# Up matmuls of 512 columns as two of 256 with the same stationary operand, in a one-core decoder layer

## The chip, the cores and the metric

The kernel runs on one core of a Trainium2 chip. The metric is the device time of one execution in microseconds (us); lower is better. The runs of the kernel before gave 2425.76 us as median of three, from 2422.67 to 2427.23. One further execution was profiled: 2423.22 us, of which the span from the first to the last instruction is 2421.1 us.

## What is computed

One decoder layer over 256 tokens of width 2048 in float32. After the attention part comes a product-key layer with 128 x 128 = 16384 single-neuron experts. This case concerns its last step:

```python
u = expert_down[et]
h = jax.nn.gelu(jnp.einsum('cd,ced->ce', xt, u), approximate=False)
vv = expert_up[et]
return jnp.einsum('ce,ced->cd', gt * h, vv)
...
h = layer_norm(ALPHA * h + y_p, ln2_g[l], ln2_b[l])
```

Each token has 128 chosen experts. The kernel doesn't gather their rows for this sum. It puts the gate values into a dense matrix G over all 16384 experts (zero where an expert isn't chosen), computes the activation A of every expert, and multiplies the product M = A * G (16384 x 256) with `expert_up` (16384 x 2048).

## The kernel before

Everything that is multiplied is streamed from HBM in tiles of 128 x 2048 float32 (two halves of 1024 columns, 512 KB each), through four raw slots. To keep float32 accuracy each number is taken apart into a high part, rounded to the format fp32r, and a low part, the rest. ScalarE (ACT) makes the high part (line 455), VectorE (DVE) the low part (line 765), and TensorE (PE) makes three products: high by high, high by low, low by high. The sync engine (SP) issues the loads (line 336).

The stages follow each other on TensorE in the order of the program:

- The projections, the attention and the query projection use `full` and `up_proj`. There the weight block of 128 x 128 is the stationary operand and the tokens are the moving one, 256 columns wide (line 1274, helper `three`). In the query projection (16 tiles, `r_hi` and `r_lo`) the moving operand has 258 columns.
- The down stage, 128 tiles in a loop of 16 passes with 8 tiles each, has pairs of a matmul of 480 columns (line 1468 or 1472) and one of 240 columns (line 1469 or 1471), 16 pairs a tile.
- The up stage, 128 tiles, turns the operands round: the stationary one is a block of M, 128 experts by 128 tokens (`m_hi`, `m_lo`, one for each half `tt` of the tokens), and the moving one is the expert tile in the weight slots. The result, 256 x 2048 float32, stays in the accumulator memory PSUM for the whole stage: it fills all eight banks of 512 columns. `up` (line 1493) takes a tile in two halves `hf` of 1024 columns, each by both `tt`, by three products `q`, by two chunks `c` of 512 columns: 24 matmuls a tile. Both chunks of a product have the same stationary operand. `first` is the first tile: it takes `tt` 1 first, since the accumulators of the down stage lie where `tt` 0 is written, and its `start` flag clears the bank ahead of the first product.

The first 8 tiles of the up stage are written out, then comes a loop of 14 passes with 8 tiles each, then 6 tiles written out. These are 126 tiles by `up`. The last two tiles go by `up_bank`, bank after bank, so that the final normalization can begin. The second half of a tile (from the third tile on) has its parts in the memory of `a_all`, which the down stage no longer needs; the first half has them in `w_first`.

In front of each tile TensorE waits for `mlo_ready` (the block of M is ready) and in front of each half for `lo_ready`. The last matmul of a half gives `half_used`, on which ACT and DVE wait to refill a slot, DVE also to make the next block of M (lines 1172, 1177, with ACT's line 673 between them).

Of the kernel before, what the change touches and what calls it, by code (L numbers as in the profile page):

```python
# [34 lines left out]
D = 2048  # L35
# [29 lines left out]
HALF = 1024  # L65
# [76 lines left out]
def build(nc, stream, x_t, const_in, small_in, keys_t, ln2, rows_dram, y_out, a_dram, g_dram):  # L142
# [92 lines left out]
    ps = ctx.enter_context(nc.psum_tensor("ps", [P, 8 * 512], F32))  # L235
# [43 lines left out]
    def weights(t, hf, moved=False):  # L279

        return (up_hi[:, t.par, :], up_lo[:, t.par, :]) if moved and hf else (w_hi[t.slot(hf)], w_lo[t.slot(hf)])
# [982 lines left out]
    def _(pe):  # L1264
        pe.sem_inc(half_used, HALVES_FREE)

        def half_ready(t, hf):
            pe.wait_ge(lo_ready, t.half(hf) + 1 + HALVES_FREE)
# [171 lines left out]
        for g in range(8):  # L1440
            tt, c0 = g % 2, 4 * (g // 2)
# [3 lines left out]
            for c in range(4):  # L1445
                ins = pe.matmul(spare[g % 4][:, P * c:P * c + P], qp[:, c0 + c, P * tt:P * tt + P], keys[:, (c0 + c) % 2, :],  # L1446
                                start=True, stop=True)
            ins.then_inc(sc_mm, 1)
        for g in range(8):
            tt, c0 = g % 2, 4 * (g // 2)  # L1450
            pe.wait_ge(sc_ready, g + 5) if g < 4 else pe.wait_ge(ht_ready, g - 3)
            pe.wait_ge(h1_ready, c0 + 4)
            for c in range(4):
                ins = pe.transpose(spare[g % 4][:, P * c:P * c + P], res[:, c0 + c, P * tt:P * tt + P], ident)
# [25 lines left out]
        def up(t, n, b, moved=True, first=False):  # L1480
            pe.wait_ge(mlo_ready, n + 1)
            for hf in range(2):
                half_ready(t, hf)
                high, low = weights(t, hf, moved)
                for tt in (1, 0) if first else range(TT):
                    s = slice(P * tt, P * tt + P)
                    if first and hf == 0 and tt == 0:
                        for u in (Tile(T_UP - 2), Tile(T_UP - 1)):
                            pe.wait_ge(acc_free[u.par], u.pair + 2)
                    for q, (m, w) in enumerate(((m_hi, high), (m_hi, low), (m_lo, high))):  # L1490
                        for c in range(2):
                            o = D * tt + HALF * hf + 512 * c
                            ins = pe.matmul(ps[:, o:o + 512], m[:, b % 2, s], w[:, 512 * c:512 * c + 512],  # L1493
                                            start=first and q == 0, stop=False, skip_group_check=True)
                ins.then_inc(half_used, 1)

        def up_bank(t, b, tt, c):

            s = slice(P * tt, P * tt + P)
            o = D * tt + 512 * c  # L1500
            w = slice(512 * (c % 2), 512 * (c % 2) + 512)
            high, low = weights(t, c // 2, True)
            pe.matmul(ps[:, o:o + 512], m_hi[:, b % 2, s], high[:, w], start=False, stop=False, skip_group_check=True)
            pe.matmul(ps[:, o:o + 512], m_hi[:, b % 2, s], low[:, w], start=False, stop=False, skip_group_check=True)
            return pe.matmul(ps[:, o:o + 512], m_lo[:, b % 2, s], high[:, w], start=False, stop=False, skip_group_check=True)

        for b in range(8):
            up(Tile(T_UP + b), b, b, b > 1, b == 0)
        with pe.Fori(1, NKEYS // 8 - 1) as i:
            for b in range(8):  # L1510
                up(Tile(T_UP + b, i, 8), i * 8 + b, b)
        for b in range(6):
            up(Tile(T_UP + NKEYS - 8 + b), NKEYS - 8 + b, b)
        last = (Tile(N_TILES - 2), Tile(N_TILES - 1))
        for b, t in enumerate(last):
            pe.wait_ge(mlo_ready, NKEYS - 1 + b)
            for c in range(4):
                if c % 2 == 0:
                    half_ready(t, c // 2)
                ins = up_bank(t, b, 0, c)  # L1520
# [92 lines left out]
```

## Time and profile before

| | |
|---|---|
| runs of the kernel before | 2422.67 to 2427.23 us, median 2425.76 us |
| profiled execution | 2423.22 us, span 2421.1 us |
| granted TensorE clock | 0.998 |
| TensorE matmul (PE) busy | 2398.4 us, 99% |
| TensorE weight load (PEld) busy | 2202.7 us, 91% |
| DVE, ACT, POOL busy | 65%, 49%, 24% |
| chain of work that ended last | 99% TensorE; line 1274 38%, line 1493 29%, line 1468 17% |

The end of a matmul in the trace is modelled: a row of 390 ns for a matmul doesn't mean that the next one starts 390 ns later. Where matmuls follow each other, the pace is the distance from start to start, or a stretch of time divided by the matmuls in it. A timeline row merges several matmuls ("x4") and gives the start of the first. PEld is the load of a stationary operand; each matmul has one, also where the operand is the same as before.

### The profile page before, as it was taken

To read this page: it belongs to the slowest core of one execution; us is meant where nothing else is said; L and a number is where in the kernel's file an instruction comes from. 1 tells how busy PE (TensorE), PEld (TensorE's weight loads), DVE (VectorE), ACT (ScalarE), POOL (GpSimd) and SP (SyncE) were. 2 spreads that over 40 slices of the span, in tenths; PEclk is the share of its full clock that TensorE was granted. 3 is DMA by queue.
4 is the path that set the end of the run, shared out by engine and by line. 5 is a ranking of instruction groups with operands and counts; after the bars stand their busy time and mean duration, and the time that the engine had idled before them with its cause. 6 is when DMAs were issued, how large, how long until landed. Compare 5 with 4: busy or idle time off the path is not lost.

```text
span 2421.1 us, 45160 instructions
## 1 busy us (share of the span) xinstructions
PE 2398.4 (99%) x15884; PEld 2202.7 (91%) x15884; DVE 1567.7 (65%) x2615; ACT 1196.5 (49%) x1787; POOL 589.8 (24%) x427
## 2 busy tenths in 40 slices
PE   8999999999999999999999999999999999999997
PEld 8999999999999999999999999999888888888886
DVE  5555555546666666888878887755655555555556
ACT  4444444545454444665556565444444444444444
POOL 0000000000000000487568886786000000000000
PEclk9999999999999999999999999999999999999999
DMA  7667666564545665688788899988776677677764
GB/s 271 217 218 227 214 230 207 182 195 149 164 148 174 194 196 178 200 219 229 220 262 259 251 275 292 280 222 260 243 244 232 236 244 243 232 238 242 243 232 145
DMA packets 182918, 539.01 MB, mean 223 GB/s; under 512 B 53664, under 2 KB 53664, under 8 KB 180432
## 3 DMA queue, kind: packets, MB, share of 16 engines
q1 hardware_dynamic: 124128, 449.89, 56.2%
q0 software_dynamic: 54128, 71.68, 12.0%
q10 hardware_dynamic: 4608, 16.78, 2.3%
q8 instruction: 26, 0.43, 0.1%
q14 instruction: 28, 0.23, 0.0%
HBM read 501.42 MB, written 35.78 MB: 222 GB/s over the span
## 4 chain that ended last, share of the span: by engine, by line
PE 99%; DVE 1%; DMA 0%; ACT 0%; issue 0%; DVEq 0%
PE ps L1274 38%; PE ps L1493 29%; PE ps L1468 17%; PE ps L1469 9%; PE ps L1472 1%; PE ps L1313 1%; PE ps L1471 1%; PE ps L1328 1%; PE ps L1321 0%; PE ps L1315 0%; PE ps L1446 0%; PE ps L1329 0%; PE ps L1308 0%; DVE u_s L1227 0%; DVE u_s L1237 0%; DVE y_s L1214 0%
## 5 line engine op out<-in xcount | busy, mean ns | idle before, releaser
L765 DVE TENSOR_TENSOR w_first<-raw,w_first 128x1024 fp32r<-128x1024 f32 x425 | 520.8, 1225 | 366.7 <-ACT w_first L455 364.6
L390 POOL DMA_INDIRECT g_dram<-lists x256 | 439.3, 1716 | 98.4 <-issue 81.8
L455 ACT ACTIVATE w_first<-raw 128x1024 fp32r<-128x1024 f32 x425 | 447.4, 1053 | 1.5 <-DMA raw<-stream 0.6
L765 DVE TENSOR_TENSOR w_second<-raw,w_second 128x1024 fp32r<-128x1024 f32 x299 | 365.9, 1224 | 2.2 <-ACT w_second L455 2.1
L1468 PE MATMUL ps<-a_all,w_first 128*128 128x480 f32 x1024 | 345.7, 384 | 0.0
L1274 PE MATMUL ps<-a_all,w_first 128*128 128x256 f32 x2520 | 314.5, 281 | 9.0 <-DVE w_first L765 9.0
L455 ACT ACTIVATE w_second<-raw 128x1024 fp32r<-128x1024 f32 x299 | 314.4, 1052 | 2.9 <-DMA raw<-stream 2.5
L1274 PEld LDWEIGHTS ps<-a_all,w_first 128*128 128x128 f32 x2520 | 299.0, 189 | 10.0 <-issue 9.0
L1274 PE MATMUL ps<-a_all,w_second 128*128 128x256 f32 x2520 | 304.5, 277 | 0.2 <-DVE a_all L796 0.2
L1468 PE MATMUL ps<-a_all,w_second 128*128 128x480 f32 x896 | 302.1, 382 | 0.0
L1274 PEld LDWEIGHTS ps<-a_all,w_second 128*128 128x128 f32 x2520 | 294.5, 188 | 0.4 <-DVE a_all L796 0.4
L1469 PE MATMUL ps<-a_all,w_first 128*128 128x240 f32 x1024 | 278.4, 272 | 0.0
L1493 PE MATMUL ps<-w_first,m_hi 128*128 128x512 f32 x1008 | 270.9, 391 | 0.0
L1493 PE MATMUL ps<-a_all,m_hi 128*128 128x512 f32 x992 | 266.5, 390 | 0.0
L765 DVE TENSOR_TENSOR a_all<-raw,a_all 128x1024 fp32r<-128x1024 f32 x126 | 154.6, 1227 | 156.7 <-ACT a_all L455 156.7
L1469 PE MATMUL ps<-a_all,w_second 128*128 128x240 f32 x896 | 243.9, 272 | 0.0
L1493 PEld LDWEIGHTS ps<-w_first,m_hi 128*128 128x128 f32 x1008 | 189.2, 188 | 41.7
L1493 PEld LDWEIGHTS ps<-a_all,m_hi 128*128 128x128 f32 x992 | 186.3, 188 | 41.0
L455 ACT ACTIVATE a_all<-raw 128x1024 fp32r<-128x1024 f32 x126 | 133.4, 1059 | 177.3 <-PE ps L1493 177.3
L1468 PEld LDWEIGHTS ps<-a_all,w_first 128*128 128x128 f32 x1024 | 192.6, 188 | 28.0
L1469 PEld LDWEIGHTS ps<-a_all,w_first 128*128 128x128 f32 x1024 | 194.0, 189 | 4.3
L678 ACT ACTIVATE part<-ps 128x240 f32<-128x240 f32 x128 | 47.7, 373 | 295.5 <-PE ps L1472 295.5
(230 smaller groups left out, 3519.7 us busy)
## 6 DMA issues: line engine op xcount, KB each, us to landing
raw<-stream SPq DMA_DIRECT2D x850, 512.0 KB, 4.3
g_dram<-blank POOLq DMA_DIRECT2D x32, 512.0 KB, 6.1
a_dram<-act ACTq DMA_DIRECT2D x32, 512.0 KB, 3.7
a_in<-a_dram POOLq DMA_DIRECT2D x32, 512.0 KB, 5.1
g_in<-g_dram POOLq DMA_DIRECT2D x32, 512.0 KB, 6.3
g_dram<-lists POOLq DMA_INDIRECT x256
res<-x_t SPq DMA_DIRECT2D x4, 512.0 KB, 6.8
ln_s<-ln POOLq DMA_DIRECT2D x1, 2048.0 KB, 7.1
```

Source lines behind the costliest of these rows:

```text
L390: pool.indirect_dma_start(out=g_cell, out_offset=bass.IndirectOffsetOnAxis(ap=lists[0:n, tt, 1, j, c:c + 1], axis=0), in_=lists[0:n, tt, 2 ...
L455: act.activation(weights(t, hf, moved)[0], raw[:, t.slot(hf), :], ACT.Copy).then_inc(hi_ready, 1)
L678: act.activation(part[:, t.par, :], acc[t.par][:, DENSE:2 * DENSE], ACT.Copy).then_inc(part_ready, 1)
L765: dve.tensor_tensor(low, raw[:, s, :], high.bitcast(F32), ALU.subtract).then_inc(lo_ready, 1)
L1274: ins = pe.matmul(out, w, a, start=first and q == 0, stop=last and q == 2)
L1313: ins = pe.matmul(ps_s[:, o:o + k1], q_s[:, q0:q0 + P], k_s[:, 0:k1], start=True, stop=not rope)
L1328: pe.matmul(ps_o[:, 0:T], v_s[:, 0, :], p_t[:, 0:T], start=True, stop=False, skip_group_check=True)
L1468: pe.matmul(both, wh, a_all[:, kk, 0:2 * DENSE], start=kk == 0, stop=False)
L1469: ins = pe.matmul(high, wl, a_all[:, kk, 0:DENSE], start=False, stop=False)
L1471: pe.matmul(high, wl, a_all[:, kk, 0:DENSE], start=False, stop=False)
L1472: ins = pe.matmul(both, wh, a_all[:, kk, 0:2 * DENSE], start=False, stop=True)
L1493: ins = pe.matmul(ps[:, o:o + 512], m[:, b % 2, s], w[:, 512 * c:512 * c + 512], start=first and q == 0, stop=False, skip_group_check=True)
```

## The change

In `up`, each matmul of 512 columns becomes two of 256 columns that follow each other, with the same stationary operand, into the two halves of the same bank. In the first tile the `start` flag, which clears the whole bank, stands only on the first of the two; the second writes where the bank has been cleared. The last matmul of a half still gives `half_used`. `up_bank` isn't changed, nor any other engine's program.

```diff
                     for q, (m, w) in enumerate(((m_hi, high), (m_hi, low), (m_lo, high))):
-                        for c in range(2):
-                            o = D * tt + HALF * hf + 512 * c
-                            ins = pe.matmul(ps[:, o:o + 512], m[:, b % 2, s], w[:, 512 * c:512 * c + 512],
-                                            start=first and q == 0, stop=False, skip_group_check=True)
+                        for c in range(4):
+                            o = D * tt + HALF * hf + 256 * c
+                            ins = pe.matmul(ps[:, o:o + 256], m[:, b % 2, s], w[:, 256 * c:256 * c + 256],
+                                            start=first and q == 0 and c % 2 == 0, stop=False, skip_group_check=True)
                 ins.then_inc(half_used, 1)
```

TensorE's order where the loop of the down stage ends and the first tile of the up stage begins, before:

```order
L1475 COMPARE_AND_BRANCH
L1493 MATMUL ps<-w_first,m_hi 128x512 x4
L1493 MATMUL ps<-w_first,m_lo 128x512 x2
L1493 MATMUL ps<-w_first,m_hi 128x512 x4
L1493 MATMUL ps<-w_first,m_lo 128x512 x2
L1493 MATMUL ps<-w_second,m_hi 128x512 x4
```

and now:

```order
L1475 COMPARE_AND_BRANCH
L1493 MATMUL ps<-w_first,m_hi 128x256 x8
L1493 MATMUL ps<-w_first,m_lo 128x256 x4
L1493 MATMUL ps<-w_first,m_hi 128x256 x8
L1493 MATMUL ps<-w_first,m_lo 128x256 x4
L1493 MATMUL ps<-w_second,m_hi 128x256 x8
```

Nothing has moved: each row has twice the matmuls at half the width. In the text of the program TensorE has 3734 matmuls where it had 3206; the loop of the up stage has 384 of them in a pass of its body where it had 192.

## Rows read from the trace of the kernel before

**Rows 1.** The page: share of each engine, and the chain that ended last.
```profile
PE 2398.4 (99%) x15884; PEld 2202.7 (91%) x15884; DVE 1567.7 (65%) x2615; ACT 1196.5 (49%) x1787; POOL 589.8 (24%) x427
...
PE 99%; DVE 1%; DMA 0%; ACT 0%; issue 0%; DVEq 0%
```

**Rows 2.** The chain from 1704 us on: start us, us, what.
```profile
1704.43 692.29 PE ps L1493 x3024
```

**Rows 3.** Stretches of 60 us in the up stage, line 1493 alone; columns as named.
```profile
core 0: us, PE busy (x) PEld busy (x), PEclk, DMA share, GB/s
1800.00:1860.00 60.00, 60.00 (x264) 49.24 (x263) 1.00 0.71 240
2300.00:2360.00 60.00, 60.00 (x264) 49.23 (x263) 1.00 0.68 232
```

**Rows 4.** Timeline of PE in the attention output projection: start us, us, engine, line.
```profile
801.74 2.88 PE L1274 MATMUL ps<-a_all,w_first 128*128 128x256 f32 x24
804.46 0.62 PE L1274 MATMUL ps<-a_all,w_second 128*128 128x256 f32 x4
```

**Rows 5.** Timeline of PEld at the same place: the weight loads.
```profile
801.63 2.79 PEld L1274 LDWEIGHTS ps<-a_all,w_first 128*128 128x128 f32 x24
804.35 0.64 PEld L1274 LDWEIGHTS ps<-a_all,w_second 128*128 128x128 f32 x5
```

**Rows 6.** Timeline of PE in the query projection, 258 columns.
```profile
945.37 0.28 PE L1274 MATMUL ps<-r_lo,w_first 128*128 128x258 f32 x1
...
946.93 0.28 PE L1274 MATMUL ps<-r_hi,w_first 128*128 128x258 f32 x1
```

**Rows 7.** Timeline from the last down tile into the first up tile, all engines.
```profile
1698.98 0.38 PE L1468 MATMUL ps<-a_all,w_first 128*128 128x480 f32 x1
...
1703.83 0.27 PE L1469 MATMUL ps<-a_all,w_second 128*128 128x240 f32 x1
...
1703.94 0.27 PE L1471 MATMUL ps<-a_all,w_second 128*128 128x240 f32 x1
...
1704.05 0.38 PE L1472 MATMUL ps<-a_all,w_second 128*128 128x480 f32 x1
...
1704.27 1.12 PE L1493 MATMUL ps<-w_first,m_hi 128*128 128x512 f32 x4
...
1704.87 0.41 DVE L1117 TENSOR_TENSOR part<-ps,part 128x240 f32<-128x240 f32 x1 [0.40 <-ACT part L678]
...
1705.68 1.08 PE L1493 MATMUL ps<-w_first,m_hi 128*128 128x512 f32 x4
```

**Rows 8.** Waits within 1750 to 2390 us: engine, line waited for, us, times, longest.
```profile
ACT m_hi L673 <- DVE m_f L1172: 190.6, 117, 1.6
ACT a_all L455 <- PE ps L1493: 164.9, 116, 1.5
DVE a_all L765 <- ACT a_all L455: 146.9, 117, 1.3
```

**Rows 9.** Timeline where the loop of the up stage begins, all engines.
```profile
1745.34 0.42 DVE L1172 TENSOR_TENSOR m_f<-a_in,g_in 128x256 f32<-128x256 f32 x1
...
1746.24 0.42 DVE L1177 TENSOR_TENSOR m_lo<-m_f,m_hi 128x256 fp32r<-128x256 f32 x1 [0.48 <-ACT m_hi L673]
...
1748.34 1.07 PE L1493 MATMUL ps<-w_first,m_hi 128*128 128x512 f32 x4
```

**Rows 10.** The page's DMA queues: packets, MB, share of 16 engines.
```profile
q8 instruction: 26, 0.43, 0.1%
```

## The prediction

> **What bounds the kernel now.** I began with the page. TensorE is busy 99% of the span and holds 99% of the chain that ended last [rows 1]. The reader is to see there that only the pace of TensorE can move the time by much, and that a busy share of 99% says nothing about that pace. The chain has one piece for the whole of `up`: 3024 matmuls in 692.29 us, without a gap [rows 2]. The count is right, 126 tiles with 24 matmuls. So one matmul of 512 columns takes 692.29 / 3024 = **228.9 ns** from start to start. Two stretches of 60 us, 500 us apart, have the same count (264 each) at a granted clock of 1.00 [rows 3]: the pace is steady and no clock effect is in it.
>
> Next I asked whether anything feeds this stage late. DMA moves 232 to 240 GB/s at a share of about 0.7 [rows 3]. ACT's longest waits in this stage are for DVE and for TensorE itself: 164.9 us in 116 waits until a half has been used; DVE in its turn waits for ACT [rows 8]. The next block of M is ready at 1746.24 + 0.42 = 1746.66 us and is wanted at 1748.34 us, 1.7 us later [rows 9]. So everyone else waits for TensorE, and the stage is 3024 times the pace of a matmul.
>
> **The change, part by part.** It removes 3024 matmuls of 512 columns and adds 6048 of 256, each with its own load of the stationary operand. The one number wanted is the pace of a matmul of 256 columns in this place. The trace has no such matmul in the up stage, so I bound it by neighbours.
>
> The nearest row is the same shape elsewhere: fp32r, 128x128 stationary, 256 columns. In the output projection 24 matmuls start between 801.74 and 804.46 us: 2.72 us / 24 = **113.3 ns** [rows 4]. The operands differ (there the weights are stationary and the tokens move), and there all matmuls of a tile add to the same columns. The loads keep up: 24 loads start in 804.35 - 801.63 = 2.72 us too, at the same 113.3 ns [rows 5]. So a new load for every 256 columns has been carried at this pace, which matters, since the change doubles the loads from one in 228.9 ns to one in 113 ns. By this row two halves take 226.7 ns, 2.27 ns less than the one of 512: 3024 x (226.7 - 228.9) = **-6.9 us** (with 113.33 and 228.93 before rounding).
>
> The low bound is the matmul of 240 columns in the down stage: 0.11 us from the first one's start to the next, twice in a row [rows 7], so about 110 ns. Two halves can hardly be quicker than two of these: 220 ns, 3024 x (220 - 228.9) = -27 us. I don't take it, because it has 16 columns fewer, and a row with just 256 exists.
>
> The high bounds are three. First, the 258-column matmuls of the query projection: 13 of them in 946.93 - 945.37 = 1.56 us, 120.0 ns each [rows 6]. That is 6.7 ns more for 2 columns more. Two of those: 240.0 ns, 3024 x 11.1 = +34 us. Second, the down stage's cost for a column: a tile of 16 pairs runs from 1698.98 to 1704.27 us, 5.29 us / 16 = 330.6 ns for 720 columns, 0.459 ns a column [rows 7]; 256 columns make 117.6 ns, two 235.1 ns, 3024 x 6.2 = +19 us. Third, a straight line (fixed cost a, cost b for a column) through the up and the down stage: a + 512 b = 228.9 and 2a + 720 b = 330.6 give b = 0.418 ns and a = 14.7 ns. Then each added matmul costs 14.7 ns, 3024 x 14.7 = +44 us.
>
> Why I take 113.3 ns against that line: it would make 256 columns 121.8 ns, and the trace has thousands at 113.3. The 258-column row suggests a step just above 256 columns: cost doesn't grow evenly, and 256 lies on the cheap side of the step. If 480 and 512 columns lie beyond it and pay for it, all these rows agree without a cost for each instruction. That is a reading of four paces and not a mechanism that I can see.
>
> A rule of the Trainium skill speaks against the change. It has no part in the sum. TensorE: Matmul & The Clock Gate, section "Back-to-back issue gap", gives N / 2.4 + 2.5 ns for a matmul of N columns: 215.8 ns for 512 and 218.3 ns for two of 256. By that rule every added matmul costs 2.5 ns, 7.6 us in all, an estimate from that page. The trace doesn't have its figures: 228.9 and 113.3 ns are both above it, by 13.1 and 4.1 ns.
>
> **Edits at nothing.** The bank is changed after two matmuls instead of after one; both ways the next result goes elsewhere, and the stage ran at an even pace [rows 3]. The start of the stage: the first tile takes `tt` 1 first, 6 matmuls of 512 columns, and then needs what DVE reads of the down accumulators. DVE is done at 1704.87 + 0.41 = 1705.28 us and TensorE gets there at 1705.68 us [rows 7]. With 12 x 113.3 = 1.36 us instead of 1.37 us nothing changes; the cover is 0.4 us. What comes late next, if TensorE is quicker by 24 x 2.27 = 54 ns a tile: the block of M with its cover of 1.7 us [rows 9]. It isn't used up. DVE, ACT, POOL and SP have the same programs.
>
> Instructions: the body of the up loop grows from 192 to 384 matmuls; the largest body so far is the down loop's with 256. Code is fetched in packets, 26 of them in the run for 0.43 MB, at 0.1% of 16 engines' span: 0.001 x 16 x 2421 / 26 = about 1.5 us each [rows 10]. I put this at nothing, because the page's chain has 0% for issue [rows 1] although the program has loops of up to 256 matmuls.
>
> **The sum.** The profiled execution took 2423.22 us, 2.5 us under the median of the runs. Less 6.9 us it would be 2416.4 us; the median of 2425.76 us would be **2418.9 us**.
>
> **Rivals.**
> 1. *Cost by columns.* In this stage a column costs 228.9 / 512 = 0.447 ns, whatever the width. Then 256 columns take 114.5 ns and nothing changes: 2425.8 us. For it: between 256 and 512 columns the cost per column differs by 1% only (0.443 and 0.447 ns). Against it: 240 columns at 110 ns are 0.458 ns a column.
> 2. *The load beside the stream is dear here* (slower). Beside 512 columns a load is in work for part of the time: PEld is busy 49.2 of 60 us [rows 3]; now there is always one. If a matmul in this stage is slowed while the next operand comes in, 256 columns cost 117.6 to 120.0 ns, by the rows of the down stage and of the query projection: +19 to +34 us, 2445 to 2459 us. It decides from 114.5 ns on. Against it: in the projections the loads follow each other at 113.3 ns and the matmuls with them [rows 4, 5].
> 3. *A fixed cost for each matmul* (slower): 14.7 ns by the line through both stages, +44 us, 2470 us. Against it stand the 256-column rows, for it that both neighbours on the time axis lie on it.
> 4. *The jump back of a longer loop* (slower). If the body no longer stays on the chip, each of 13 jumps back waits for a packet, 13 x 1.5 = +20 us on top of the -6.9: 2439 us; if three packets each time, more. The Trainium skill bears on this in Runtime: NRT & Kernel Launch, section "Instruction fetch mechanics": a taken branch whose target isn't in the window stalls, but TensorE's instruction memory is given as 2048 instructions, and a body of 384 matmuls with their loads is under 800. By its size no stall would come; no run here has shown it.
>
> **How the numbers follow.** Forecast (113.3 ns): 0.52. Rival 1: 0.12. Rival 2: 0.16. Rival 3: 0.10. Rival 4: 0.10. About 0.2%, 4.9 us, is what a measurement of this kernel can tell from no change. The forecast's gain is 0.28%, so I leave 0.04 of its 0.52 to "same": faster 0.48, same 0.17, slower 0.35. The range goes from 2413 us (a little more than the forecast's gain) to 2452 us: that takes in rival 1, rival 4 and the lower half of rival 2, and leaves out rival 3, the upper half of rival 2 and a gain toward the 240-column bound, together under 0.2. The forecast's own range is 2415 to 2421 us.
>
> **What would show it.** In the profile after, the chain should have 6048 matmuls on line 1493 in about 685.4 us: 113.3 ns each, 529 or 530 starts in a stretch of 60 us, weight loads at the same pace, no idle time of TensorE. Rival 1 is right if the piece stays at 692 us. With rival 2 or 3 the pace is an even 118 to 122 ns with nobody waited for. With rival 4 the pace within a pass is 113.3 ns, and a gap of over 1 us stands once in eight tiles, with more than 26 packets of code. ACT should still wait for TensorE in each tile. A clock under 1.00 in the stage, or a shift in the other stages, would make the prediction wrong in a way that I don't foresee.

## The result and the profile after

| | before | after |
|---|---|---|
| time, us | 2424.22, median of 4 runs (2422.27 to 2427.23) | 2442.89, median of 4 runs (2442.51 to 2446.23) |
| profiled execution, us | 2423.22 | 2443.16 |
| its span, us | 2421.1 | 2441.0 |
| mean granted clock | 0.998 | 0.998 |

The changed kernel is slower by 0.84%: the ratio of its time to the time before is 1.0084, with a 95% interval of 1.0073 to 1.0096, or 18 to 23 us. I had forecast a gain of 6.9 us.

The page after, its row of engines and its chain (they answer to [rows 1]):

```profile
PE 2418.3 (99%) x18908; PEld 2346.9 (96%) x18908; DVE 1567.3 (64%) x2615; ACT 1196.7 (49%) x1787; POOL 592.8 (24%) x427
...
PE 99%; DVE 1%; DMA 0%; ACT 0%; issue 0%; DVEq 0%
```

TensorE has 3024 matmuls more and nothing else has changed on this level: it still holds 99% of the span and of the chain. The chain from 1704 us on (start us, us, what) shows where the time is; it answers to [rows 2]:

```profile
1704.27 712.35 PE ps L1493 x6048
```

The piece was 692.29 us and is 712.35 us: +20.06 us, and the profiled executions differ by 19.94 us. So the whole difference lies in this one piece, and the same sum shows that nothing else moved. One matmul of 256 columns takes 712.35 / 6048 = **117.8 ns** here; two take 235.6 ns, where the one of 512 took 228.9.

Stretches of the up stage after, line 1493 alone (columns as in [rows 3]: stretch, length, PE and PEld busy with counts, granted clock, DMA share, GB/s), and one stretch of the output projection, line 1274:

```profile
core 0: us, PE busy (x) PEld busy (x), PEclk, DMA share, GB/s
1800.00:1860.00 60.00, 60.00 (x512) 60.00 (x511) 1.00 0.67 228
2300.00:2360.00 60.00, 60.00 (x512) 60.00 (x511) 1.00 0.68 237
...
770.00:830.00 60.00, 60.00 (x532) 60.00 (x531) 1.00 0.59 193
```

The pace is even: 512 in both stretches of the stage (a count includes those that run over an edge). My forecast wanted 529 or 530 starts, and with the two at the edges that is the 532 of the projection, where the same shape runs as before. The clock is full in all three, so the two paces, 117.8 and 113.3 ns, are no matter of the clock.

Nobody feeds the stage late. In 1750 to 2400 us ACT waits for TensorE (us, times, longest) as in [rows 8], a little longer than the 164.9 us there, and the queue of code packets has 30 of them where [rows 10] has 26:

```profile
ACT a_all L455 <- PE ps L1493: 183.7, 116, 1.7
...
q8 instruction: 30, 0.49, 0.1%
```

The four packets more cost nothing that can be seen: the chain is one piece, issue has 0% of it, and there is no idle time of TensorE between passes of the loop. The rule that I had weighed in the prediction, of a stall at a taken branch whose target isn't in the window (the Trainium skill, Runtime: NRT & Kernel Launch, "Instruction fetch mechanics"), doesn't show here with a body of 384 matmuls.

The timeline at the stage's start (start us, us, engine, line), beside [rows 7]:

```profile
1704.11 1.13 PE L1493 MATMUL ps<-w_first,m_hi 128*128 128x256 f32 x8
...
1704.71 0.41 DVE L1117 TENSOR_TENSOR part<-ps,part 128x240 f32<-128x240 f32 x1 [0.40 <-ACT part L678]
...
1705.55 1.10 PE L1493 MATMUL ps<-w_first,m_hi 128*128 128x256 f32 x8
```

DVE is done at 1705.12 us and TensorE comes at 1705.55 us: the cover of 0.4 us held. But from 1704.11 to 1705.55 us 12 matmuls start, 120 ns each with the first, longer step: the pace is off from the first tile on.

So the question is why the shape that takes 113.3 ns in the projections takes 117.8 ns here.

### The profile page after: what moved, and what is told of

The parts are those of the page before. It is cut to its first block, busy times and chain, and to the rows that moved or that the text cites. A ratio compares the mean times of both kernels' runs of the same rounds, so it can differ in the third digit from the quotient of the medians.

```text
span 2441.0 us, 51208 instructions
## 1 busy us (share of the span) xinstructions
PE 2418.3 (99%) x18908; PEld 2346.9 (96%) x18908; DVE 1567.3 (64%) x2615; ACT 1196.7 (49%) x1787; POOL 592.8 (24%) x427
## 4 chain that ended last, share of the span: by engine, by line
PE 99%; DVE 1%; DMA 0%; ACT 0%; issue 0%; DVEq 0%
PE ps L1274 38%; PE ps L1493 29%; PE ps L1468 17%; PE ps L1469 9%; PE ps L1472 1%; PE ps L1313 1%; PE ps L1471 1%; PE ps L1328 1%; PE ps L1321 0%; PE ps L1315 0%; PE ps L1446 0%; PE ps L1329 0%; PE ps L1308 0%; DVE u_s L1227 0%; DVE u_s L1237 0%; DVE y_s L1214 0%
## 5 line engine op out<-in xcount | busy, mean ns | idle before, releaser
L1274 PEld LDWEIGHTS ps<-a_all,w_second 128*128 128x128 f32 x2520 | 294.2, 188 | 0.4 <-DVE a_all L796 0.4
L1493 PE MATMUL ps<-w_first,m_hi 128*128 128x256 f32 x2016 | 278.0, 279 | 0.0
L1493 PE MATMUL ps<-a_all,m_hi 128*128 128x256 f32 x1984 | 273.6, 279 | 0.0
L1493 PEld LDWEIGHTS ps<-w_first,m_hi 128*128 128x128 f32 x2016 | 255.0, 188 | 0.1
L1493 PEld LDWEIGHTS ps<-a_all,m_hi 128*128 128x128 f32 x1984 | 251.0, 188 | 0.0
L1468 PEld LDWEIGHTS ps<-a_all,w_second 128*128 128x128 f32 x896 | 168.6, 188 | 27.6
```

What stands on the lines that cost most here:

```text
L1274: ins = pe.matmul(out, w, a, start=first and q == 0, stop=last and q == 2)
L1468: pe.matmul(both, wh, a_all[:, kk, 0:2 * DENSE], start=kk == 0, stop=False)
L1493: ins = pe.matmul(ps[:, o:o + 256], m[:, b % 2, s], w[:, 256 * c:256 * c + 256], start=first and q == 0 and c % 2 == 0, stop=False, skip_g ...
```

## The experiments

### Is it the company, the form or the place?

Four theories stood at first; the letters are those of the expectations. A: every matmul has a fixed cost, 6.7 ns, and each column 0.434 ns (the line through 228.9 ns for 512 columns and 117.8 ns for 256). B: the company does it (transfers, other engines at work). C: the place of the results or of the operands sets the pace. D: the load of the stationary operand sets a floor.

**Probes on a quiet core.** Behind the last output, when no one else works, 24 matmuls each of one width, then variants of one thing at 512 and at 256 columns.

```diff
+        pe.wait_ge(out_ready, 4 * TT)
+        def probe(w, m, o, n, step=0, mstep=0, wstep=0, count=24):
+            for k in range(count):
+                oo, mo, wo = o + step * (k % 2), mstep * (k % 2), wstep * (k % 2)
+                pe.matmul(ps[:, oo:oo + n], w[:, wo:wo + P], m[:, mo:mo + n], start=True, stop=True, skip_group_check=True)
+        for n in (512, 480, 448, 384, 320, 288, 272, 258, 256, 240, 224, 192, 128, 64):
+            probe(mh, w_hi[0], 0, n)
...
+            probe(w_hi[0], a_flat[:, 0:1024], 0, n, wstep=128)
+            probe(mh, w_hi[0], 0, n, step=512, mstep=512, wstep=256)
```

> The kernel before, and behind its last output blocks of 24 matmuls each on a quiet core (no DVE, ACT or stream at work), one row of the timeline for each block; their results are used by nobody. First a sweep of widths from 512 to 64 columns with m_hi stationary and an expert tile moving, as in the up stage; then 512 and 256 columns with one thing changed at a time: destination bank alternating, moving operand alternating, stationary operand alternating, moving operand in other memory, stationary operand from a weight slot, all three alternating. Theory A (a fixed cost of 6.7 ns for each matmul and 0.434 ns for a column, the line through 228.9 ns for 512 and 117.8 ns for 256 columns in the up stage): 256 columns take 117.8 ns and 512 take 228.9 ns here too, 384 take 173 ns, 128 take 62 ns unless the load of the stationary operand needs more. Theory B (the 0.434 ns for a column come from what the other engines and the stream do to TensorE's reads or writes in the stage): on the quiet core 256 columns take 113.3 ns and 512 take 220 ns or less. Theory C (where the operands lie or whether the destination changes decides): one of the alternations or places moves 256 columns from 113.3 to 117.8 ns. Theory D (the load sets a floor): all widths under some 256 columns take the same 110 to 118 ns.

The groups of the sweep (by form: count, busy us, mean ns of one). Busy time covers 23 steps and one whole matmul, so the pace is (busy - mean) / 23:

```profile
L1532 PE MATMUL ps<-w_first,m_hi 128*128 128x480 f32 x24 | 5.4, 380 | 0.0
...
L1532 PE MATMUL ps<-w_first,m_hi 128*128 128x384 f32 x24 | 4.3, 336 | 0.0
L1532 PE MATMUL ps<-w_first,m_hi 128*128 128x320 f32 x24 | 3.7, 307 | 0.0
...
L1532 PE MATMUL ps<-w_first,m_hi 128*128 128x258 f32 x24 | 3.0, 282 | 0.0
L1532 PE MATMUL ps<-w_first,m_hi 128*128 128x256 f32 x24 | 3.0, 279 | 0.0
L1532 PE MATMUL ps<-w_first,m_hi 128*128 128x240 f32 x24 | 2.8, 274 | 0.0
...
L1532 PE MATMUL ps<-w_first,m_hi 128*128 128x128 f32 x24 | 2.8, 274 | 0.0
L1532 PE MATMUL ps<-w_first,m_hi 128*128 128x64 f32 x24 | 2.8, 276 | 0.0
```

That gives 218 ns for 480 columns, 172 for 384, 147 for 320, 118 for 258 and for 256, and 110 ns for 240, 128 and 64 alike (within 2 ns each). Two things are new. There is no step at 256 columns: 258 and 256 differ by no more than that reading's 2 ns. And from 240 columns down there is a floor of 110 ns. My low bound, 110 ns for 240 columns, was this floor.

The quiet core has the pace of the up stage: about 118 ns for the up stage's own operands at 256 columns, with no transfer under way (share 0.00). B falls. The variants, from the timeline (start us, us, line, count) of those that follow each other:

```profile
2526.53 14.24 PE L1532 MATMUL ps<-w_first,m_hi 128*128 128x512 f32 x96
2540.61 2.99 PE L1532 MATMUL ps<-w_second,m_hi 128*128 128x256 f32 x24
2543.43 5.87 PE L1532 MATMUL ps<-a_all,m_hi 128*128 128x256 f32 x48
2549.14 5.78 PE L1532 MATMUL ps<-a_all,w_first 128*128 128x256 f32 x48
2554.75 2.88 PE L1532 MATMUL ps<-w_first,m_hi 128*128 128x256 f32 x24
```

The row of 2540.61 has 24 starts in 2543.43 - 2540.61 = 2.82 us, 117.5 ns. The last row has the same kinds of operands as the first 256-column probes, and 23 steps in 2.88 - 0.28 = 2.60 us: 113 ns. **One form has two paces.** Changing one thing at a time (the bank of the result, the moving operand, the stationary operand) left 229 and 117.8 ns. The last row alternates all three at once, so the probes alone don't exclude that the combination does it; the swapped kernel below settles that. The two rows of 48 between them mix two probes each, and their means are 119.0 and 116.9 ns: a third pace, 120.0 ns, is in both, for the probes whose two operands start at the same offset within 128 bytes (the start of `a_all` with `m_hi`; `w_first` with the up stage's part of `a_all`, which begins 64 bytes behind its start). At 512 columns the same probes were the quicker ones. Two stretches of PE (columns: stretch, length, busy with count, clock, DMA share, GB/s), the first in such a probe, the second in one with `w_first` stationary and the start of `a_all` moving:

```profile
2511.00:2515.00 4.00, 4.00 (x20) 1.00 0.00 0
...
2523.00:2526.00 3.00, 3.00 (x14) 1.00 0.00 0
```

By the starts within them these are 226.7 ns and 233.3 ns. The operands of the second probe gave 113.4 ns at 256 columns: what is quick for one width is slow for the other. I come back to this below.

**All results into one place.** After, with every pass of the loop adding to the same 256 columns.

```diff
-                            o = D * tt + HALF * hf + 256 * c
+                            o = D * tt + HALF * hf + 256 * c if not one else 0
```

> The changed kernel, but in the 14 passes of the loop every matmul of the up stage adds into the same 256 columns of one bank, as a tile of the projections does (the sums of those 112 tiles are lost). Theory C, destination: 113.3 ns a matmul in the loop, 112 x 48 x 4.45 ns = 24 us less than the changed kernel, about 2417 us in the profiled execution. Theories A and B: 117.8 ns as before, 2441 us in span.

2446.38 us. The chain:

```profile
1707.38 712.35 PE ps L1493 x6048
```

The same 712.35 us: the place of the results isn't it.

**The roles swapped.** After, the loop's passes with the expert's tile stationary and M moving, as the projections have it.

```diff
+                            if swap:
+                                ins = pe.matmul(ps[:, o:o + 256], w[:, g:g + P], m[:, b % 2, :],
+                                                start=False, stop=False, skip_group_check=True)
```

> The changed kernel, but in the 14 passes of the loop the operands change roles: the expert tile is stationary in blocks of 128 x 128, the block of M moves with its 256 columns, as in the projections; 48 matmuls of 256 columns a tile as before (the loop's sums come out transposed, so in the wrong places). If the roles or the memory of the operands decide, 113.3 ns a matmul and about 24 us less than the changed kernel; if the stage's company decides (theory B), 117.8 ns and no change.

2417.52 us. The chain, with line 1498 for the normal roles (8 tiles ahead of the loop, 6 behind) and 1495 for the swapped ones:

```profile
1703.94 45.05 PE ps L1498 x384
1748.99 609.30 PE ps L1495 x5376
2358.29 32.64 PE ps L1498 x288
```

The first line is 117.3 ns a matmul, the second 113.3 ns, and the third, the old form again, 32.64 / 288 = **113.3 ns**. That fits neither A nor C: the form that was slow ahead of the loop is quick behind it. The pace is carried on from what ran before, as on the quiet core. The swapped form took only two matmuls to reach 113.3 ns.

The first line isn't one pace either. In the first two tiles the halves in `w_second` ran at 113.5 ns and everything else at 117.8 ns; on return to `w_first` the pace fell back.

**384 and 128 instead of 256 and 256.**

```diff
-                        for c in range(4):
-                            o = D * tt + HALF * hf + 256 * c
+                        for c, (at, n2) in enumerate(((0, 384), (384, 128), (512, 384), (896, 128))):
+                            o = D * tt + HALF * hf + at
```

> The change with other sizes: each 512 columns as 384 and 128. By theory A without a floor the two take 173.3 + 62.2 = 235.6 ns, as two of 256 do, and the time is that of the changed kernel, +20 us to before. With a floor of about 110 ns under each matmul (theory D) the pair takes 173 + 110 = 283 ns, 3024 x 54 ns = +164 us to before, about 2588 us.

2596.0 us, 173.5 us more than before beside it. The chain:

```profile
1702.57 866.85 PE ps L1493 x6048
```

The pair takes 286.7 ns; the probes gave 172 + 110 = 282 ns, and without a floor A wanted 235.6 ns. So 128 columns save nothing against 240: the floor holds in the stage too. A split with a narrow part is dear, at any pace.

### What decides which pace is held?

Theory E: the pace is a state that lasts while matmuls follow each other. The down stage leaves TensorE in the slow one, and a stop lets it enter the quick one. Theory F, which came later: there are two paces for one stream, a stop can end in either, and either lasts until something disturbs it.

**A short stop ahead of the stage**, with 256 and with 512 columns: TensorE waits for its own last matmul of the down stage.

```diff
             pe.wait_ge(mlo_ready, n + 1)
+            if first:
+                pe.wait_ge(half_used, Tile(T_UP - 1).half(1) + 1 + HALVES_FREE)
```

> The changed kernel with one more wait: ahead of the first matmul of the up stage TensorE waits until its own last matmul of the down stage has counted as done, a stop of some 0.2 to 0.4 us. Theory E (the pace is a state of TensorE's pipeline that lasts while matmuls follow each other: the down stage leaves it in a slow one, 117.8 ns for 256 columns, a stop lets it fall into the quick one, 113.3 ns): the whole stage runs at 113.3 ns, 6048 x 4.45 = 27 us less than the changed kernel and 6.9 us less than the kernel before, about 2417 us. Theory A (fixed cost for each matmul): 117.8 ns, 2443 us as the changed kernel.

2446.49 us, ratio 1.0087 (1.0070 to 1.0104); 712.56 us for the 6048 matmuls, the slow pace.

> The kernel before, matmuls of 512 columns, with the same one wait ahead of the up stage. Theory E: 512 columns have a quick pace too, 226.7 ns (seen once on the quiet core) in place of 228.9, 3024 x 2.27 = 6.9 us less than before, and some 0.3 us of stop: about 2417.5 us. Theory A: 228.9 ns, no change but the stop.

2426.55 us, ratio 1.0006 (0.9997 to 1.0016); 692.50 us, 229 ns. A short stop changes neither pace, against E.

**A longer stop**: the first tile in its natural order, so that TensorE waits about 1 us for the down accumulators to be read.

```diff
-                for tt in (1, 0) if first else range(TT):
+                for tt in range(TT):
```

> The changed kernel, the first up tile in the natural order of the token halves, so that TensorE waits about 1 us for the accumulators of the down stage to be read. Theory E: 113.3 ns from then on, about 2418 us. Theory A: 117.8 ns, about 2444 us.

2443.64 us. The timeline of TensorE behind the stop:

```profile
1704.73 1.15 PE L1493 MATMUL ps<-w_first,m_hi 128*128 128x256 f32 x8 [0.99 <-DVE part L1117]
1705.72 0.62 PE L1493 MATMUL ps<-w_first,m_lo 128*128 128x256 f32 x4
1706.17 1.07 PE L1493 MATMUL ps<-w_first,m_hi 128*128 128x256 f32 x8
...
1707.53 1.11 PE L1493 MATMUL ps<-w_second,m_hi 128*128 128x256 f32 x8
1708.47 0.63 PE L1493 MATMUL ps<-w_second,m_lo 128*128 128x256 f32 x4
```

From 1705.72 to 1707.53 us 16 matmuls start in 1.81 us: 113.1 ns. From 1707.53 on 8 start in 0.94 us: 117.5 ns. The quick pace was there for half a tile and was gone with the switch to `w_second`. It came back once, in the half of the second tile that lies in `w_second` (8 matmuls in 0.91 us from 1713.19 us on), and went with the next switch. Then the stage stayed slow; the piece is 712.36 us.

**Is it where w_second lies?** The same, with the gap of 128 bytes ahead of `w_second` moved behind it.

```diff
-    sb("gap_w", [P, 32])
     w_second = sb("w_second", [P, 2, 2, HALF], F32R)
+    sb("gap_w", [P, 32])
```

> The changed kernel with the long stop of about 1 us at the start of the up stage, which gave 113.3 ns until the first switch to w_second, and with the gap of 128 bytes between w_first and w_second moved behind w_second. Theory F with the offset as the disturbance: 113.3 ns through the first tiles and, if nothing else disturbs it, through the stage, about 2418 us. If the switch itself disturbs and not the offset: 117.8 ns from the second half of the first tile on. The other stages may change by a few us through the new addresses.

2440.74 us, 712.56 us for the piece: the slow pace from the first tile on. It didn't help. And the stop was the same 0.99 us, with the same operands at the same places behind it (`w_first` and `m_hi` haven't moved): the half tile that had 113.1 ns in the run before had 117.8 ns here, on another chip. So a stop of 1 us, too, was followed once by either pace.

**Pairs as in the down stage, put into a projection**: before, with 8 pairs of 480 and 240 columns between the second and third tile of a projection.

```diff
+        for k in range(8):
+            pe.matmul(ps_o[:, 0:480], a_all[:, k, 0:P], a_all[:, k + 1, 0:480], start=True, stop=True)
+            pe.matmul(ps_o[:, 0:240], a_all[:, k, P:2 * P], a_all[:, k + 1, 0:240], start=True, stop=True)
```

> The kernel before, with 8 pairs of a 480-column and a 240-column matmul put between the second and the third tile of the mix projection (their result goes to a bank that nobody reads); 2.6 us of work. There TensorE runs at 113.3 ns for 256 columns before and after. Theory E: behind the pairs the 256-column matmuls may stay at 117.8 to 120 ns until TensorE next stops, 14 tiles x 48 x 4.5 ns = +3 us on top of the 2.6. Theories A and C: 113.3 ns on both sides.

2429.45 us in one execution, 3.2 us more than the median of before beside it, whose own executions lie 6.7 us apart; so the timeline has to tell. The pairs alone take 2.6 us. They are 326 ns each, where the down stage has 330.6 ns (here both operands lie in `a_all`), so they weren't quite that stage's stream. Behind them:

```profile
851.38 0.28 PE L1274 MATMUL ps<-b_hi,w_first 128*128 128x256 f32 x1
...
851.97 0.39 PE L1274 MATMUL ps<-b_hi,w_first 128*128 128x256 f32 x2
...
852.99 0.28 PE L1274 MATMUL ps<-b_hi,w_first 128*128 128x256 f32 x1
```

Five matmuls start between 851.38 and 851.97 us, 118 ns each, and the next nine in 1.02 us, 113.3 ns. In a projection the quick pace is back after five matmuls, without a stop, as it was after two in the swapped kernel. E falls as I had put it: the slow pace doesn't last everywhere until TensorE stops. But projections aren't free of it, as the trace of the kernel before shows (further down).

### A stop inside the stage

**A wait of 2.5 us ahead of the third tile**, for the second half of the tile behind it.

```diff
             pe.wait_ge(mlo_ready, n + 1)
+            if isinstance(n, int) and n == 2:
+                half_ready(t.next(), 1)
```

> The changed kernel; TensorE stops ahead of the third up tile until a half of the fourth is ready, about 2.5 us. From that tile on only w_first and a_all are moving operands. Theory F (TensorE has two paces for one and the same stream of 256-column matmuls, 113.3 and 117.8 ns, either lasts until something disturbs it; the switch from w_first to w_second disturbs it, the switch from w_first to a_all does not): if the stop ends in the quick pace it stays for the 124 tiles that follow, 124 x 48 x 4.45 = 26.5 us less than the changed kernel, about 2419 us; a stop can also end in the slow one, as in the kernel with the short stop, then about 2446 us. What theory A (a fixed cost for a matmul) expects is 117.8 ns whatever is done.

2419.04 us in one execution, 3.6 us less than before beside it (2422.63, from 2420.25 to 2427.41). Timeline and chain:

```profile
1717.63 1.15 PE L1495 MATMUL ps<-w_first,m_hi 128*128 128x256 f32 x8 [2.51 <-issue]
...
1717.63 674.80 PE ps L1495 x5952
```

Here the whole rest of the stage, 124 tiles, ran at 674.80 / 5952 = 113.4 ns. The forecast's pace is possible in this stage, with its operands, its company and its loops.

**The same kernel again**, on another chip.

> The kernel with the stop of 2.8 us ahead of the third up tile again, timed in five rounds. Theory F, if the quick pace is entered each time: every execution near 2419 us, some 4 us under the kernel before in the same rounds, ratio 0.998. If the entry is left to chance from run to run: some executions at 2419 and some at 2446 us.

2446.83 us (2446.61 to 2447.02, 4 runs), ratio 1.0101 (1.0085 to 1.0118). Timeline ahead of the stop and behind it, chain, and the stretch of TensorE behind the stop:

```profile
1713.66 1.07 PE L1495 MATMUL ps<-w_second,m_hi 128*128 128x256 f32 x8
1714.57 0.62 PE L1495 MATMUL ps<-w_second,m_lo 128*128 128x256 f32 x4
1717.70 2.04 PE L1495 MATMUL ps<-w_first,m_hi 128*128 128x256 f32 x8 [2.51 <-issue]
...
1717.70 702.59 PE ps L1495 x5952
...
1717.00:1720.00 3.00, 2.30 (x11) 0.55 0.69 228
```

This time the rest of the stage has 702.59 / 5952 = 118.0 ns, which is 117.8 ns behind a start at about half pace: right behind the stop the granted clock was 0.55, for the most part the 1.2 GHz level. In the run before, the clock behind the same stop of 2.51 us was 1.00. So the stop didn't decide it by itself, and it isn't a means that can be relied on. I can't say whether the chip or the clock made the difference.

The two runs differed ahead of the stop already. Here the half tile in `w_second` has eight matmuls in 1714.57 - 1713.66 = 0.91 us, 113.5 ns by all its starts; in the run before the same eight took 0.94 us, 117.7 ns. The instructions and addresses up to there are the same. Five kernels that have the first two tiles in this form were profiled on this chip. Four of them had the quick pace in both `w_second` halves: this one, the swapped one and the two with short stops below. The one with all results in one place hadn't. So the chip alone doesn't set it, and the same instructions can meet either pace.

**The same stop with 512 columns.**

> The kernel before, matmuls of 512 columns, with the stop of 2.5 to 2.8 us ahead of the third up tile. If 512 columns have a quick pace of 226.7 ns as well: 124 x 24 x 2.27 = 6.7 us less and 2.7 us for the stop, 4 us under the kernel before. If they have the one pace of 228.9 ns: 2.7 us over it.

2427.35 us, ratio 1.0022 (1.0012 to 1.0032): half clock behind the stop here too (0.50 from 1717 to 1720 us), then 229 ns. It costs the stop and brings nothing.

**Short stops inside the stage.** TensorE waits for its own last matmul ahead of the third tile, and in another kernel ahead of each of 124 tiles.

```diff
+            if isinstance(n, int) and n == 2:
+                pe.wait_ge(half_used, t.half(0) + HALVES_FREE)
```

> The changed kernel with one stop of a drain (some 0.1 to 0.2 us over the pace) ahead of the third up tile. Theory F, if the length of the stop doesn't matter: 113.3 ns for 124 tiles, about 2416.5 us, 6.5 us under the kernel before. If a stop has to be long, or ends in either pace by its phase: 117.8 ns and 2446 us.

2441.73 us, ratio 1.0087 (1.0070 to 1.0104); 701.25 us for 5952: 117.8 ns.

> The changed kernel; ahead of each up tile from the third on TensorE waits until its own matmuls have counted as done, a stop of some 75 to 200 ns over the pace, 124 times. Theory F: each stop is a new entry, so the tiles show 113.3 or 117.8 ns, tile by tile, and the share of quick ones is to be read; all quick would be 26.5 us less and 10 to 25 us of stops. Theory A: 117.8 ns in every tile and 2453 to 2468 us.

2491.55 us. Its chain within the loop, two of the tiles:

```profile
1806.00 0.12 issue
1806.12 5.93 PE ps L1495 x48
...
1812.16 5.93 PE ps L1495 x48
```

A piece of 5.93 us is 47 steps of 117.8 ns, one whole matmul of 0.28 us, and 0.1 us that the first step behind a stop takes longer: each of the stops was followed by a tile at the slow pace. A tile with its stop takes 6.05 us where 48 x 117.8 ns are 5.65 us, so a stop costs 0.4 us although the chain shows only 0.12 us of it as a gap.

**Swapped matmuls ahead of the third tile** (12 of them, expert's tile stationary, zeros moving, so that they add nothing), with 256 columns and with 512.

```diff
+            if isinstance(n, int) and n == 2:
+                pe.wait_ge(zero_ready, 1)
+                half_ready(t, 0)
+                for k in range(12):
+                    pe.matmul(ps[:, 512 * (k % 8):512 * (k % 8) + T], weights(t, 0, moved)[0][:, P * (k % 8):P * (k % 8) + P], zero[:],
+                              start=False, stop=False, skip_group_check=True)
```

> The changed kernel; ahead of the third up tile TensorE has 12 matmuls of 256 columns with the roles swapped (a block of the expert tile stationary, a tile of zeros moving), which add zero to the sums: 1.4 us. Theory F: in the kernel with swapped roles in the loop the quick pace outlasted the swap for the 6 tiles behind it, so it should hold here for 124 tiles: 26.5 us less than the changed kernel, 1.4 us more for the interlude, about 2418 us, 5 us under the kernel before. Theory A: 117.8 ns and 2444 us.

2446.36 us, ratio 1.0101 (1.0085 to 1.0118); 701.01 us for 5952, 117.8 ns. The interlude itself:

```profile
1715.19 1.56 PE L1490 MATMUL ps<-zero,w_first 128*128 128x256 f32 x12
1716.60 1.10 PE L1503 MATMUL ps<-w_first,m_hi 128*128 128x256 f32 x8
```

> The kernel before, matmuls of 512 columns, with the same interlude ahead of the third up tile. Theory F, if 512 columns have two paces as well (226.7 ns was seen once on the quiet core): 124 x 24 x 2.27 = 6.7 us less, 1.4 us more, about 2418 us in the profiled execution of a kernel before of 2423. If 512 columns have one pace in this stage: +1.4 us.

2423.98 us, ratio 1.0006 (0.9996 to 1.0016); 681.18 us for 2976, 228.9 ns. This doesn't test whether a quick pace is carried on, for there was none to carry: the twelve start in 1.41 us, 117 ns each, in both kernels, where the swapped loop had 113.3 ns from its third matmul on. So swapped roles alone don't give the quick pace. One difference is where the moving operand starts: in the program's allocation the tile of zeros lies 32 bytes off a multiple of 128 and M 64 bytes. Whether that is it, no run here tested.

### Where the operands start

In the program's allocation `w_first` and `w_second` start at multiples of 128 bytes in each partition, `m_hi` and `m_lo` 64 bytes off one. The probes said that two operands at the same offset are quicker at 512 columns and slower at 256 (theory G: the starts modulo 128 bytes choose the pace). Both kernels can be moved there by 64 bytes.

```diff
     m_f = sb("m_f", [P, 2, T], F32, up_mem)
+    sb("gap_m", [P, 16], F32, up_mem)
     m_hi = sb("m_hi", [P, 2, T], F32R, up_mem)
```

Before, with the gap:

> The kernel before with a gap of 64 bytes in front of m_hi, so that the stationary operands of the up stage (m_hi, m_lo) start at a multiple of 128 bytes, as the moving ones in w_first, w_second and a_all do. Theory G (the start addresses of the two operands, taken modulo 128 bytes, choose among the paces): 226.7 ns for 512 columns in the stage, 3024 x 2.27 = 6.9 us less, some 2416 us, ratio 0.997. If addresses don't matter in the stage: 228.9 ns and no change.

2415.86 us (2415.06 to 2416.17, 6 runs), with before beside it at 2423.35 us: ratio **0.9965** (0.9953 to 0.9977). The chain:

```profile
1703.16 685.65 PE ps L1494 x3024
```

685.65 / 3024 = 226.7 ns, 2.2 ns less than before. It is quicker than both kernels of this study, and its stage has the time, 685.4 us, that I had forecast for the split. After, with the gap:

> The changed kernel with the same gap. Theory G: 120.0 ns for 256 columns, 6048 x 2.2 = 13.5 us more than the changed kernel, about 2457 us. So the shift that helps 512 columns hurts 256. If addresses don't matter: 117.8 ns, 2443 us; if the equal start lets the quick pace win: 113.3 ns, 2416 us.

2455.56 us. The chain, and a stretch of 60 us of PE:

```profile
1703.21 725.72 PE ps L1494 x6048
...
1800.00:1860.00 60.00, 60.00 (x503) 1.00 0.65 220
```

725.72 / 6048 = 120.0 ns. One gap of 64 bytes, the work unchanged: 512 columns gain 2.2 ns, 256 columns lose 2.2 ns. The effect is shown; what in the chip makes it isn't in the trace.

But 128 bytes isn't the right measure. In the first two tiles half of the work is in `w_second`, which starts 16 KB and the gap of 128 bytes behind `w_first`. The kernel of 512 columns with the gap, in its first two tiles:

```profile
1705.76 1.09 PE L1494 MATMUL ps<-w_second,m_hi 128*128 128x512 f32 x4
...
1708.55 1.08 PE L1494 MATMUL ps<-w_first,m_hi 128*128 128x512 f32 x4
...
1711.28 1.09 PE L1494 MATMUL ps<-w_second,m_hi 128*128 128x512 f32 x4
```

The 12 matmuls in `w_second` take 2.79 us, 232.5 ns, as they did without the gap; the next 12, in `w_first`, take 2.73 us, 227.5 ns. Both start at a multiple of 128 bytes, as `m_hi` now does, but modulo 256 bytes `w_second` starts at 0 where the other two start at 128. The part of `a_all` that the stage uses starts at 128 as well, and the probes with 226.7 ns had equal starts modulo 256 too. So what all rows here bear out is equal starts modulo 256 bytes; equal modulo 128 isn't enough.

## Why the prediction was wrong

**What bounds the kernel** was right. The time moved by the pace of TensorE in one stage and by nothing else, and the sum over the chain closes to 0.1 us.

**The price of 256 columns** is the step that failed: "a row with just 256 exists". I took 113.3 ns from the output projection [rows 4], since it was the same shape. The stage gave 117.8 ns. The term was 3024 x (226.7 - 228.9) = -6.9 us; with 2 x 117.8 it is 3024 x 6.6 = +20.1 us, which is what the profiles show. The shape didn't carry its pace along: with one form there were 113 and 118 ns on a quiet core, 117.3 ahead of a loop and 113.3 behind it in the swapped kernel, and 113.4 and 118.0 ns in two runs of one kernel. I could have seen it in the trace that I had, in a projection of the kernel before:

```profile
423.40 2.99 PE L1274 MATMUL ps<-a_all,w_second 128*128 128x256 f32 x24
426.22 2.88 PE L1274 MATMUL ps<-a_all,w_first 128*128 128x256 f32 x24
```

The first 24 start in 2.82 us, 117.5 ns each; the next 24, up to 428.94 us, in 2.72 us, 113.3 ns, at a granted clock of 1.00. Most 256-column matmuls there run at 113.3 ns, but how many don't changes from run to run of the same instructions: around 60 us the kernel before has 113.3 ns, and the kernel with 512 columns and the short stop has 117.8 ns in the same tile.

**The reading of four paces**, a step just above 256 columns, failed too. On the quiet core 258 and 256 columns have the same 118 ns, and nothing steps between 256 and 480. The 120.0 ns of [rows 6] against the 113.3 ns of [rows 4] is more than two columns can cost. I had noted that the row asks for a step and that no mechanism stood behind it, and used it all the same to set the fixed cost aside.

**The bounds.** The low one (110 ns for 240 columns) was a floor and no point on a line. Among the high ones the down stage's cost for a column came out almost to the number (117.6 against 117.8 ns), but as a neighbour and not as a law: 240 columns of that stage sit on the floor. The line with a = 14.7 ns mixed a matmul on the floor with one above it. A line through the up stage's own two points, 228.9 and 117.8 ns, has a = 6.7 ns and 0.434 ns a column. It gives 173.4 ns for 384 columns and 145.6 for 320, where the probes had 172 and 147.

**The rule of the skill that spoke against the change** had the sign right. By TensorE: Matmul & The Clock Gate, "Back-to-back issue gap" in the Trainium skill each added matmul costs 2.5 ns, in a formula that the page gives for an isolated matmul; by the two traces it cost 235.6 - 228.9 = 6.6 ns. Its N / 2.4 + 2.5 for 256 columns, 109.2 ns, is below every pace of 256 columns measured here.

**The rivals.** Rival 1 (by columns) would have kept the piece at 692 us. Rival 2 had the price (117.6 to 120.0 ns) but its mechanism, the next load beside the stream, isn't shown: each 256 columns had a load of their own at 113 ns too, on the quiet core and in one run of the stage. Rival 3, a fixed cost for each matmul, had over twice the size, and no one cost fits: the added matmul cost 6.6 ns in the two kernels, 2 x 120.0 - 226.7 = 13.3 ns with the gap of 64 bytes, and less than nothing where the stage ran at 113.4 ns. Rival 4 (the loop) is out: 4 packets more, no gap.

**The edits at nothing** were right: the change of bank (the kernel with one place of results had the same 712.35 us), the start with its 0.4 us of cover, the block of M, the longer loop.

**The chances.** The range of 2413 to 2452 us held the time, but that is no merit of the mechanism: it had been drawn over the neighbours' prices. The 0.52 for the forecast was too much for a price that rested on one row from another stage, while the stage just ahead of this one spoke for a loss. A small slip besides: 0.12 for rival 1 and the 0.04 taken from the forecast make 0.16 for "same" and leave 0.36 for "slower", not 0.17 and 0.35.

**What stays open** is what decides which pace a stream holds, and what in the chip makes it. Ruled out as the cause of the slow pace: the place of the results, the company, the loop. Short stops didn't end it. A stop of 2.5 us was followed by the quick pace in one run and by the slow one in the next, and these two also differed in the chip, in the clock behind the stop, and in the pace of the `w_second` halves ahead of it. The starts of the operands matter (the gap of 64 bytes shows it), but at the starts of this stage a stream of 256 columns had either pace, and so had the projections at theirs. Which part the roles of the operands have, apart from their starts, wasn't tested: the swapped kernel changed both.

## What to carry to other kernels

Take the price of a split from the same place: the same operands, at the same addresses, behind the same stage; a row of the same shape from elsewhere leaves some 4% open, and that was more than the whole gain here. And look at more than one row: the other pace stood in the same trace. Don't cut below the floor, 110 ns here, and when a stage is nothing but TensorE's pace, try the start of its operands: 64 bytes moved this kernel by 0.35% where the split had lost 0.84%.

## What the runs showed of the hardware

- A stream of one shape holds one of several even paces under a full clock: 226.7, 228.9 and 233.3 ns for 512 columns, 113.3, 117.8 and 120.0 ns for 256.
- With both operands at the same offset within 256 bytes, 512 columns take the lowest of them (226.7 ns) and 256 the highest (120.0 ns), in the stage as on the quiet core. Equal within 128 but not within 256 bytes, 512 columns took 232.5 ns.
- The same instructions at the same addresses had 117.7 ns in one run and 113.5 ns in another, ahead of any stop.
- A matmul with its own load of the stationary operand took about 110 ns from 64 to 240 columns.
- Behind a stop of 2.5 us TensorE started once at full clock and twice (the same kernel again, and the one of 512 columns) at about half pace, at a granted clock of 0.55 and 0.50 over 3 us, which is the 1.2 GHz level for most of that stretch; behind stops of 0.1 to 1 us the matmuls kept the full pace.
